# A root-mean-square norm between two layers: the residual added in groups by two engines, the squares summed with a column of ones

## The reference, cut to what matters

```
x = x + g1 * rms_norm(y, norm_g[1])
h = rms_norm(x, norm_g[2]) * (1 + sc2) + sh2
x = x + g2 * rms_norm(sq_relu_mlp(h, mlp_up, mlp_down), norm_g[3])
# second block
h = rmsnorm(x, g_mix) * (1.0 + sc1) + sh1
```

## Time and profile before

| | us |
|---|---|
| median of 3 runs (lowest, highest) | 3307.74 (3307.04, 3309.56) |
| the profiled execution | 3307.34 |
| its span | 3305.7 |
| TensorE busy | 3227.1 (98%) |
| VectorE busy | 2204.6 (67%) |
| ScalarE busy | 1241.4 (38%) |
| GpSimd busy | 196.2 (6%) |

### The profile page before, as it was taken

The page is one execution under the profiler, slowest core; times in us unless marked ns, Lnnn a source line. Parts: engine busy times, 40 slices in busy tenths (PEclk is TensorE's granted clock), DMA queues, the critical chain, the costliest instruction groups (busy, mean ns, idle before and its releaser), DMA issues.

```text
span 3305.7 us, 58756 instructions
## 1 busy us (share of the span) xinstructions
PE 3227.1 (98%) x23408; PEld 2700.4 (82%) x23408; DVE 2204.6 (67%) x3396; ACT 1241.4 (38%) x1686; POOL 196.2 (6%) x298
## 2 busy tenths in 40 slices
PE   7999999999999999989999999989999999999998
PEld 4764685478888999978888888878888888888887
DVE  2377656665655677667878777787666667667667
ACT  2202130144444421344344444444544443443444
POOL 0000000012122000000000000000000000000000
PEclk9999999999999999999999999999999999999999
DMA  9956727622222688637767777745445557656654
GB/s 408 364 204 229 277 86 258 241 84 89 89 92 98 234 353 349 228 140 258 276 244 271 256 256 259 255 169 180 161 153 178 191 190 261 210 190 241 225 179 156
DMA packets 101013, 709.02 MB, mean 214 GB/s; under 512 B 11200, under 2 KB 11328, under 8 KB 19520
## 3 DMA queue, kind: packets, MB, share of 16 engines
q1 hardware_dynamic: 73872, 525.89, 43.9%
q0 software_dynamic: 23184, 169.88, 13.9%
q10 hardware_dynamic: 3744, 10.23, 0.8%
HBM read 698.36 MB, written 7.60 MB: 214 GB/s over the span
## 4 chain that ended last, share of the span: by engine, by line
PE 92%; DVE 4%; DMA 2%; issue 1%; ACT 1%; DVEq 0%; SPq 0%; ACTq 0%; POOLq 0%
PE ps L2704 33%; PE ps L2703 17%; PE ps L632 11%; PE ps L2407 3%; PE ps L1099 3%; PE ps L399 2%; PE ps L2700 2%; PE ps L1819 2%; PE ps L1100 2%; PE ps L1101 2%; PE ps L1833 1%; PE ps L2389 1%; PE ps L2388 1%; PE ps L2390 1%; PE ps L1091 1%; PE ps L2701 1%
## 5 line engine op out<-in xcount | busy, mean ns | idle before, releaser
L2704 PE MATMUL ps<-hT_parts,rows_parts 128*128 128x512 f32 x3210 | 1130.6, 394 | 0.0
L2703 PE MATMUL ps<-hT_parts,ring_parts 128*128 128x256 f32 x3210 | 901.9, 281 | 1.7 <-DVE hT_parts L2676 1.6
L2667 DVE TENSOR_TENSOR ring_parts<-ring,rows_parts 128x2048 fp32r<-128x2048 f32 (+1 forms) x337 | 762.1, 2262 | 102.7 <-ACT rows_parts L2662 101.7
L2662 ACT ACTIVATE rows_parts<-ring 128x2048 fp32r<-128x2048 f32 (+1 forms) x337 | 639.4, 1897 | 406.2 <-DMA ring<-in_mlp_u 209.1
L2704 PEld LDWEIGHTS ps<-hT_parts,rows_parts 128*128 128x128 f32 x3210 | 604.2, 188 | 125.0
L2703 PEld LDWEIGHTS ps<-hT_parts,ring_parts 128*128 128x128 f32 x3210 | 607.9, 189 | 12.6 <-DVE hT_parts L2676 2.9
L2704 PE MATMUL ps<-work_parts,rows_parts 128*128 128x512 f32 x1616 | 570.1, 395 | 0.0
L2703 PE MATMUL ps<-work_parts,ring_parts 128*128 128x256 f32 x1616 | 454.2, 281 | 0.0
L632 PE MATMUL ps<-hT,ring 128*128 128x512 f32 (+1 forms) x1088 | 372.4, 505 | 0.0
L2704 PEld LDWEIGHTS ps<-work_parts,rows_parts 128*128 128x128 f32 x1616 | 304.2, 188 | 63.2
L632 PEld LDWEIGHTS ps<-hT,ring 128*128 128x128 f32 x1088 | 206.9, 190 | 163.4 <-issue 152.0
(11 more groups left out here) (495 smaller groups left out, 4532.5 us busy)
## 6 DMA issues: line engine op xcount, KB each, us to landing
ring<-in_mlp_u SPq DMA_DIRECT2D x128, 1024.0 KB, 5.0
ring<-in_ffn_u SPq DMA_DIRECT2D x88, 1024.0 KB, 4.8
rows<-in_mod_r POOLq DMA_DIRECT2D x64, 1024.0 KB, 5.2
ring<-in_gate_u SPq DMA_DIRECT2D x64, 1024.0 KB, 5.2
work<-in_ada_r POOLq DMA_DIRECT2D x64, 1024.0 KB, 5.2
ring<-in_in_u SPq DMA_DIRECT2D x36, 1024.0 KB, 4.8
rows<-in_ada_r POOLq DMA_DIRECT2D x32, 1024.0 KB, 9.0
ring<-in_down_u SPq DMA_DIRECT2D x32, 1024.0 KB, 4.9
```

The source lines that it names most:

```text
L2662: act.activation(unit_high(u)[:, 0:size], slot(u)[:, 0:size], ACT.Copy).then_inc(hi_done, 1)
L2667: dve.tensor_tensor(ring_parts[:, ring_slot(u), 0:size], slot(u)[:, 0:size], unit_high(u)[:, 0:size].bitcast(F32), ALU.subtract)\
L2703: pe.matmul(ps[:, b, low_half], low, top(kt), start=False, stop=False)
L2704: mm = pe.matmul(ps[:, b, :], high, both(kt), start=False, stop=kt == kts - 1)
```

## The change

It has four parts.

1. The gain is no longer applied by VectorE. ScalarE multiplies each tile of y by its gain column in place (`scale_tile`): in turn one inside the loop of `Mix`, after the tile's square; in turn two after the MLP's loop, two tiles before the square root of y's norm and 14 behind it.
2. VectorE multiplies y by the spread roots four tiles at a time (128x1024, the second input a PSUM bank read four times), all four groups first. It then adds tiles 6 to 15 to x in four instructions (two, four, two and two tiles).
3. GpSimd adds tiles 0 to 5 to x, two at a time (`add_pairs`), as soon as their group is multiplied. ScalarE's squares wait for GpSimd's pairs first, then for VectorE's (`pair_added`). VectorE waits for GpSimd's three before it goes on, and counts them into `nadd`.
4. The second norm is summed like the first, but straight from the squares: each half tile of squares (128x128) is the stationary operand and one column of ones moves. Root and reciprocal are then taken of two columns, and TensorE spreads the result into the PSUM bank that y's norm used, from which `scale_split` reads.

```diff
             def tensor(self, pe):
                 acquire(pe, self.use)
-                if not self.summed:
+                if self.summed:
...
+                else:
                     for kt in range(KT):
                         if kt % self.step == 0:
                             pe.wait_ge(nsq, self.first + kt // self.step + 1)
-                        mm = pe.matmul(ps[:, self.use[0], 0:T], kc("ones"), self.squares[:, kt, :], start=kt == 0, stop=kt == KT - 1)
-                    mm.then_inc(bk.full[self.use[0]], 1)
-                    return
...
+                        for a in range(TT):
+                            mm = pe.matmul(ps[:, self.use[0], a:a + 1], self.squares[:, kt, a * P:(a + 1) * P], kc("ones", 0, 1),
+                                           start=kt == 0 and a == 0, stop=kt == KT - 1 and a == TT - 1)
                 mm.then_inc(bk.full[self.use[0]], 1)
                 acquire(pe, self.spread)
                 pe.wait_ge(nrs, self.k)
...
-                to, n = (root[:, 0:TT], TT) if self.summed else (rtn, T)
-                emptied(self.use, act.activation(to, ps[:, self.use[0], 0:n], ACT.Sqrt, bias=eps(EPS_RMS), scale=1.0 / D))
+                emptied(self.use, act.activation(root[:, 0:TT], ps[:, self.use[0], 0:TT], ACT.Sqrt, bias=eps(EPS_RMS), scale=1.0 / D))
...
-                dve.reciprocal(to, to).then_inc(nrs, 1)
-                if self.summed:
-                    full(dve, self.spread)
-                else:
-                    dve.wait_ge(nrs, self.k)
+                dve.reciprocal(root[:, 0:TT], root[:, 0:TT]).then_inc(nrs, 1)
+                full(dve, self.spread)
...
-        def add_scaled(dve, own, src, col, rms):
-
-            for kt in range(KT + 1):
-                if kt < KT:
-                    own.step(dve.tensor_tensor(src[:, kt, :], src[:, kt, :], rms.rows, ALU.mult))
-                if kt:
-                    own.settle(1 if kt < KT else 0)
-                    t = kt - 1
-                    dve.scalar_tensor_tensor(xT[:, t, :], src[:, t, :], col[:, t:t + 1], xT[:, t, :], ALU.mult, ALU.add).then_inc(nadd, 1)
+        POOL_PAIRS = 3
...
+        def add_pairs(pool, own, src, turn):
+
+            assert own.n == POOL_ADDED + POOL_PAIRS * turn
+            for n in range(POOL_PAIRS):
+                pool.wait_ge(dve_done, root_at[turn, n // 2])
+                both = slice(2 * n, 2 * n + 2)
+                own.step(pool.tensor_tensor(xT[:, both, :], xT[:, both, :], src[:, both, :], ALU.add))
+
+        def pair_added(eng, n, turn, before):
+
+            if n < POOL_PAIRS:
+                eng.wait_ge(pool_done, POOL_ADDED + POOL_PAIRS * turn + n + 1)
+            else:
+                eng.wait_ge(nadd, before + 2 * (n + 1 - POOL_PAIRS))
+
+        def scale_tile(act, y, gain):
+
+            act.activation(y, y, ACT.Copy, scale=gain).then_inc(merge_sum, 1)
+
+        def add_scaled(dve, own, src, rms, scaled, turn):
+
+            def times_root(g):
+
+                group = src[:, 4 * g:4 * g + 4, :]
+                dve.wait_ge(merge_sum, scaled + 4 * (g + 1))
+                own.step(dve.tensor_tensor(group, group, bc(rms.rows, 4), ALU.mult))
+                root_at[turn, g] = own.n
+
+            def add(first, last, back):
+
+                own.settle(back)
+                both = slice(first, last)
+                dve.tensor_tensor(xT[:, both, :], xT[:, both, :], src[:, both, :], ALU.add).then_inc(nadd, last - first)
+
+            for g in range(KT // 4):
+                times_root(g)
+            add(2 * POOL_PAIRS, 8, 2)
+            add(8, 12, 1)
+            add(12, 14, 0)
+            add(14, 16, 0)
+            dve.wait_ge(pool_done, POOL_ADDED + POOL_PAIRS * (1 + turn))
+            dve.wait_ge(nadd, KT * turn + KT - 2 * POOL_PAIRS)
+            dve.sem_inc(nadd, 2 * POOL_PAIRS)
             rms.read(dve)
...
                         rms_y1.square_out(act, yT1[:, t, :], sq1[:, t, :])
+                        scale_tile(act, yT1[:, t, :], gn1[:, t])
...
+                for t in range(2):
+                    scale_tile(act, yT2[:, t, :], gn3[:, t:t + 1])
                 rms_y2.scalar(act)
+                for t in range(2, KT):
+                    scale_tile(act, yT2[:, t, :], gn3[:, t:t + 1])
 
             def gpsimd(pool, own):
+                pool.wait_ge(x_again, 16)
+                add_pairs(pool, own, yT1, 0)
                 pool.wait_ge(nadd, KT)
                 pool.memset(flat(yT2), 0.0).then_inc(pool_tiles, 1)
                 pool.wait_ge(x_split, KT)
                 fetch_late(pool, 0, LATE_ROWS)
+                add_pairs(pool, own, yT2, 1)
```

More of the change, by code:

```diff
@@ L2534, in branch_kernel, with __init__ @@
         class Rms:
-            def __init__(self, src, ready, summed=0, reset=1, last=None, turns=1):
+            def __init__(self, src, ready, summed=0, reset=1, last=None, turns=1, bank=None):
                 self.src, self.ready, self.summed = src, ready, summed
@@ L2548, in __init__ @@
                 self.use = aux()
[L2549 to L2552, removed]
+                self.spread = bk.take(bank) if bank else aux()
+                self.rows = ps[:, self.spread[0], 0:T]
             def square_out(self, act, src, dst):
@@ L2572, in tensor @@
                 acquire(pe, self.use)
-                if not self.summed:
+                if self.summed:
+                    pe.wait_ge(sq_added, self.total)
+                    for a in range(TT):
+                        pe.matmul(ps[:, self.use[0], a:a + 1], sq_sum[:, a * P:(a + 1) * P], kc("ones", 0, 1), start=a == 0, stop=False)
+                    pe.wait_ge(nsq, self.first + self.summed)
+                    for a in range(TT):
+                        mm = pe.matmul(ps[:, self.use[0], a:a + 1], self.last[:, a * P:(a + 1) * P], kc("ones", 0, 1), start=False, stop=a == TT - 1)
+                else:
                     for kt in range(KT):
@@ L2610, in vector @@
-                dve.reciprocal(to, to).then_inc(nrs, 1)
-                if self.summed:
-                    full(dve, self.spread)
-                else:
-                    dve.wait_ge(nrs, self.k)
+                dve.reciprocal(root[:, 0:TT], root[:, 0:TT]).then_inc(nrs, 1)
+                full(dve, self.spread)
             def read(self, eng):
-                if self.summed:
-                    eng.sem_inc(bk.free[self.spread[0]], 1)
+                eng.sem_inc(bk.free[self.spread[0]], 1)
@@ new lines, in branch_kernel @@
+        POOL_ADDED = 4 * len(ROUNDS)
+        root_at = {}
+        def add_pairs(pool, own, src, turn):
[9 more added lines that the diff above has]
+                eng.wait_ge(nadd, before + 2 * (n + 1 - POOL_PAIRS))
@@ L2783, in wo_out @@
                         act.wait_ge(bk.free[j % 2], it * 2 + (use_wo[j % 2][1] + j // 2 + 1))
-                        rms_y1.square_out(act, yT1[:, bass.ds(it * 4 + j, 1), :], sq1[:, bass.ds(it * 4 + j, 1), :])
+                        t = bass.ds(it * 4 + j, 1)
+                        rms_y1.square_out(act, yT1[:, t, :], sq1[:, t, :])
+                        scale_tile(act, yT1[:, t, :], gn1[:, t])
                         if not last or j < 3:
@@ L2811, in vector @@
                 dve.wait_ge(x_again, 16)
-                add_scaled(dve, own, yT1, gn1, rms_y1)
+                add_scaled(dve, own, yT1, rms_y1, 2 * PAIRS2, 0)
                 rest_unit(dve, seg_mlp + AHEAD_DVE)
@@ L2924, in vector @@
                 rms_y2.vector(dve)
-                add_scaled(dve, own, yT2, gn3, rms_y2)
+                add_scaled(dve, own, yT2, rms_y2, 2 * PAIRS2 + KT, 1)
         gmix, gffn = coef[:, 0:KT], coef[:, KT:2 * KT]
```

5 lines of the change are left out of this document (2 added, 3 removed).

## The result

| | median of its runs (lowest, highest) | runs |
|---|---|---|
| changed kernel | 3315.66 us (3313.14, 3324.89) | 12 |
| kernel before, beside it | 3309.28 us (3305.02, 3312.36) | 12 |

The ratio is 1.0024, with a 95% interval of 1.0017 to 1.0031. The change makes the kernel 6.4 us slower. Its profiled execution took 3313.18 us (span 3311.5), 5.84 more than the one before.

What follows compares the result with a forecast made beforehand. TensorE holds 92% of the chain, so time moves only where it waits or slows; VectorE paces both turns. 3.0 + 4.15 + 1.4 = 8.5 us on 3307.34 or the median 3307.74 gives 3316; range 3304 to 3319.

Steps and rivals of the forecast that it cites:

- The sum, the term that decides: Second norm's sum in both turns: 64 passes 0.21 us apart at half clock, 13.4 us, and 0.25 to land.
- Scaling later by 3.0 and 4.15: Start of scaling behind the second norm: 3.0 us later in turn one, 4.15 in turn two.
- VectorE, 7.5 us: VectorE's new products and adds in a turn: 7.5 us against 11.6, so 4 us less.
- GpSimd, 1.27 a pair: GpSimd's three adds of 128x512 to x: 1.27 us each, as beside VectorE's final products.
- The third rival: GpSimd holds the chain: a pair takes 2.5 us instead of 1.27, total 3320.5; chance 0.03.
- ScalarE, 0.40 a scaling: ScalarE's gain scalings: 0.40 us each; turn two's 14 behind the root put the first square at 2202.5.
- Paired products, 0.6 and 0.8 more: Paired products behind the two turns: 13.6 us each, 0.6 and 0.8 more than before.
- the slow spell of 5 us: Half clock after the sum, over the paired products: 5 us taken, between 3.0 and 6.8.
- 11.3 plus half the slow time: Rule for the paired products' length, read from both turns before: 11.3 us plus half the half-clock time.
- The rival that the clock returns: Clock returns inside the sum; scaling 1.4 and 1.3 us earlier; 3302 to 3305, main value 3304.6; chance 0.13.
- The rival that the sum is never the bound: Loads 0.11 apart at any clock, or clock never falls; scaling 4.5 and 4.6 us earlier; 3298.6; chance 0.06.
- by that rule the sum would never bind: Skill's load price, 107 ns at either clock level: the sum would never bind and the change would win.

Runs made afterwards that it cites:

- e1: Changed kernel, but each of the 64 matmuls of a norm's sum moves 128 columns of ones instead of one; 3305.11 us.
- e7: Changed kernel's one-column sum plus unread 256-column matmuls in TensorE's idle time (2, 8 and 4); 3308.97 us.
- e4: e1 plus unread 256-column matmuls in TensorE's idle time: 2 and 8 ahead of the sums, 4 behind; 3301.71 us.
- e10: e6 plus 10 more unread 256-column matmuls between the sum and the first scaled product; 3303.68 us.
- e6: e5 plus unread 256-column matmuls in TensorE's idle time, 2 and 8 ahead of the sums; 3302.48 us.
- e5: Changed kernel with the running norm's sum back at 256 moving columns against a block of ones, both in float32r; 3301.57 us.
- e3: Kernel before with only the new sum (64 loads, one column of ones), residuals as before; 3314.50 us.

## Why the prediction came out right, and where it was off

The forecast of 3316 stands against 3315.66, by the mechanism named. That it comes within 0.4 us is luck: two of its terms were off in opposite ways, and so was the median that they were added to.

- **The sum, the term that decides.** Forecast: passes 0.21 us apart at half clock, 13.4 us and 0.25, the clock down throughout. Measured: (13.73 - 0.33) / 63 = 0.213 apart, 13.8 us, PEclk 0.50 to the end in both turns. e1 shows that the width is the reason (0.21 to 0.11 with 128 columns), e7 that one column even loses the clock. The step rested on one stretch of narrow matmuls, and that reading was good.
- **Scaling later by 3.0 and 4.15.** Measured 3.20 and 4.32. The excess lies mostly between the sum's end and scaling, 1.87 and 1.94 us against 1.7: the four spreading passes took 1.19 at half clock (0.68 at full, for y's root of turn one), 0.5 more and not 0.4. In turn two the clock fell already at 2197.60, and VectorE's first product waited 1.38 us for the spread instead of 0.87. I had not seen that a spell could reach back there, but it held nobody: the first square waited for ScalarE's scalings.
- **VectorE, 7.5 us.** Measured 4.61 + 3.47 = 8.1. Products of 1024 columns took 1.15 each, as read from the earlier trace rows; the adds were undersized. Nothing hung on it behind that sum. "The 4 us that VectorE gives back are lost behind it": the squares ended 3.4 and 2.9 us sooner and idle times of 8.25 and 8.93 us stood behind them.
- **GpSimd, 1.27 a pair.** Measured 3.74 and 3.73 for three, 1.27 for a single one. The third rival falls.
- **ScalarE, 0.40 a scaling.** Measured 5.68 / 14 = 0.41. The first square of turn two started 5.75 behind the root, against a forecast of 5.86 (2202.5 - 2196.64).
- **Paired products, 0.6 and 0.8 more: mis-sized.** Measured 12.9 and 12.9 us, against 13.0 and 12.8 before: nothing more. The step that failed is the slow spell of 5 us, taken from the third turn: the clock was back 3.3 and 3.8 us after the first product (1474.13 to 1477.40, 2221.12 to 2224.90), about as before. The rule beside it, "11.3 plus half the slow time", lacks a floor. VectorE's 32 instructions take 12.7 us (first scaling 20.43 behind the root, last one done at 33.13), and the products end 1.6 behind them at best, 12.5 after the first product, as e1 and e4 show at PEclk 1.00; only where the first product came late, 0.6 and 1.0 in e7 and 2.8 and 3.6 in e10, did they take less, 11.9, 11.8 and 11.3. So a slow spell of 3.3 us costs 0.4, and one of 5.1 us costs 1.3 (e6). With its 5 us the prediction's own rule gives 13.8, not 13.6; it had put 11.1 for the 11.3.
- **The sum of the terms** was 8.5, the turns measured 7.5, the medians 6.4. The number came out so near since I put 8.5 on a median of 3307.7, and the difference was 6.4 on one of 3309.3.
- **The rival that the clock returns** forecast 3304.6 and is a kernel of its own: e1, at 3305.11. The rival that the sum is never the bound (3298.6) was mis-worked. With loads 0.11 apart its own numbers end the sum at 1460.09 + 7.04 + 0.25 = 1467.4, 0.9 later than it took (1465.4 + 0.88 + 0.25), and in turn two at 2203.3 + 7.04 + 0.25 = 2210.6, so that scaling comes 3.8 and 2.6 sooner than before, not 4.5 and 4.6: 3301.3. e4, with loads 0.11 apart throughout, came at 3301.71, and its sum was still the bound. A sum that isn't one is e5's, at 3301.57; there the wide root and reciprocal cost 2.35 us from sum to scaling, against 1.37 in e4.

Part of the loss is not the sum's pace but its late start (0.77 and 1.75 us, after against e3). The forecast had it in its first squares without telling it apart. What it did not see is that the old sum is about as dear for TensorE.

The Trainium skill (TensorE: Matmul & The Clock Gate, section "LDWEIGHTS (loading the stationary operand)") prices a load at its columns over 1.2 GHz and has no term for the clock's level: an estimate of 107 ns for 128 columns. The runs agree at PEclk 1.00 (0.11 in e4) and differ at 0.50 (0.213 after the change): the measurement decides. The prediction's "by that rule the sum would never bind" doesn't follow even so: with loads 0.11 apart e4's sum ends 2.4 and 2.8 us behind the last square.

## What to carry to other kernels

Before a reduction over partitions is turned round, count its passes in TensorE's time at both clocks, and ask what moves: a long stream of weight loads with one column fell to half clock here, and stayed there, though TensorE was never idle. A gain ahead of a bound that starts with the first item is worth what it does to the first item, not to the last. Fillers are worth their place only where TensorE's pace counts; elsewhere they move the slow spell or hold the next product.

## What the runs showed of the hardware

- The granted clock fell from 1.00 to 0.50 in the midst of 64 one-column matmuls with TensorE busy 5.00 of the 5.00 us ahead of the fall (e7, turn two), and came back in the midst of the same stream with 128 columns (e1, both turns).
- A 256-column matmul against ones took, start to start, 0.21 us in float32 at full clock and 0.43 at half, and a float32 tile is two of these. In float32r a tile is one, and the shortest step at half clock was 0.21 us (1465.72 to 1465.93, 2201.13 to 2201.34 in e5). So the sum's work at half clock falls from 13.7 us to 16 x 0.21 = 3.4, an estimate: no run had sixteen of them without a gap.
- VectorE's 128x1024 products and GpSimd's 128x512 adds ran side by side without a sign of each other: 1.27 us a pair of tiles on GpSimd after the change, and 1.27 in the earlier trace rows.
